# State products of four chunks issued as one group over four row groups in a chunked gated-recurrence layer

## Chip, cores and metric

One Trainium2 chip, all 8 cores, each with 4 of the 32 sequences; no core talks to another. The metric is the device time of the slowest core in microseconds (us). PE is TensorE (the matmul engine), DVE is VectorE, ACT is ScalarE, POOL is GpSimd, SP is the engine that issues most transfers.

## The reference, cut to what matters

One layer on x (32, 2048, 1024) in float32. A token-mixing half: a modulated RMSNorm, one input projection to q, forget logits, v, output gate and pooling values, then a gated recurrence in four heads of 128 channels, and a pooling mixer; both go through the output projection. A channel-mixing half: RMSNorm, up projection to 4096, squared ReLU, down projection. The part around the change, with chunks of 32 tokens:

```python
k_out = k * jnp.exp(b_last - b)              # decay from s to chunk end
def step(S, xs):
    q_c, k_c, v_c, d_c = xs
    o = jnp.einsum('bhcd,bhde->bhce', q_c, S)
    S = d_c[..., None] * S + jnp.einsum('bhcd,bhce->bhde', k_c, v_c)
    return S, o
```

The state product k_c^T v_c contracts over only the 32 tokens of a chunk and gives 128 x 128 per head. The products of different chunks do not depend on each other; the update of S does.

## The kernel before

Each core works through 8192 tokens in 16 tiles (t = 0 to 15) of 512 tokens. A tile is four blocks (j) of 128 tokens, a block four chunks (c = 4j + jj) of 32 tokens. The work of a tile:

- N1: RMSNorm and transposes into `ucT` (`norm_to_T`).
- A: input projection; per head the decays; `koutT` transposed to `koutk` (tokens on partitions), `scT` (scores), `qin`; v and the pooling values token by token (`vtok`, `ptok`).
- B (`stage_B`): `pool_j` and `pool_g` (the pooling mixer, PSUM banks 6 and 7), then for each block `chain(j)` and `oT(j)`. `chain` forms for each chunk the four heads' state products (PE, rows `pb<-vtok,koutk`), updates the float32 state with four multiply-adds (DVE, `S<-S,decs,pb`), and casts the state to bfloat16 (ACT, `Sbf<-S`). `oT` forms the block's outputs from scores and states (PE, rows `pb<-scT,vtok` and `pb<-qin,Sbf`), squares them (ACT, `osq`), averages over a head with a matmul by ones (PE, `pb<-osq,cbt`), takes Ln and Exp (ACT, `rsb`), and multiplies (DVE, `rsb<-pb,rsb`, the last read of the output's bank, then `ucT<-rsb,gnwc,sg`).
- C: output projection from `ucT` (PE, rows `pb<-wsl,ucT` with 512 columns) and gated residual add.
- N2: norm and transposes into `u2T`.
- UP: 32 groups of eight matmuls (`pb<-u2T,wsl`), each followed by a ReLU in place on DVE (`pb<-pb`) and a square on ACT (`hidT<-pb`). DOWN: 256 matmuls (`pb<-wsl,hidT`). OUT: final norm and store.

UP and DOWN use PSUM banks 0 to 3 in turn, everything of the mixing half banks 4 to 7. In `chain` the banks of the products alternate between 4 and 5 by chunk; `oT` puts its output into bank 6 or 7 and the averages into bank 4 or 5.

The order on each engine is not written by hand. The program lists its operations with their reads, writes, an assumed duration (`dur`) and a priority (`P.base`, then place in the list); a list scheduler (`Prog.schedule`) then simulates the engines and picks on each, whenever it is free, the ready operation of lowest priority value. Tile t+1's mixing half (base 10(t+1)) and tile t's UP and DOWN (base 10t + 15) are in play together, so MLP matmuls fill PE wherever the mixing half waits; the mixing half goes first where both are ready. Every PSUM bank is one buffer to the scheduler: a group that writes it waits for the last reader of what was there. The order found is fixed in the program; on the chip each engine runs it in order and waits on semaphores. Weights come through two rings of four slots (`wsl`), from float32 in the first tile (with a conversion by POOL's transfers) and from a bfloat16 copy afterwards. Only tile 0's mixing half has no MLP work beside it, and only tile 15's MLP has no mixing half.

Many operations are recorded by helpers: L480 is `mm` (all matmuls but transposes), L483 `tr`, L486 `actf`, L490 and L491 `ts`, L494 `tt`, L497 `stt`, L500 `cp`.

Of the kernel before, what the change touches and what calls it, by code (L numbers as in the profile page):

```python
# [17 lines left out]
TT = 512  # L18
# [281 lines left out]
def V(t, off, dims, p0=0, n=128):  # L300
    row = 1
    for s in t.shape[1:]:
        row *= s
    return bass.AP(t, p0 * row + off, [[row, n]] + [list(d) for d in dims])
# [23 lines left out]
def build_nc(NT=NT_FULL):  # L328
# [32 lines left out]
    with ExitStack() as st:  # L361
        def sb(name, shape, dt):
            return st.enter_context(nc.sbuf_tensor(name, list(shape), dt))
# [15 lines left out]
        vtok = sb("vtok", [128, 4, TT], BF16)  # L379
# [3 lines left out]
        koutk = sb("koutk", [128, 4, TT], BF16)  # L383
# [29 lines left out]
        pb = [st.enter_context(nc.psum_tensor("pb%d" % i, [128, 512], F32)) for i in range(8)]  # L413
# [13 lines left out]
        P = Prog()  # L427

        def bufs(name, n, **k):
            return [Buf("%s%d" % (name, i), **k) for i in range(n)]  # L430
# [15 lines left out]
        B_v = bufs("v", 4)  # L446
# [3 lines left out]
        B_koutk = bufs("koutk", 4)  # L450
# [9 lines left out]
        B_pb = bufs("pb", 8, excl=True)  # L460
# [18 lines left out]
        def mm(out, lhsT, rhs, start, stop, **k):  # L479
            return lambda e: e.matmul(out, lhsT=lhsT, rhs=rhs, start=start, stop=stop, **k)  # L480
# [4 lines left out]
        def actf(out, in_, func, **k):  # L485
            return lambda e: e.activation(out=out, in_=in_, func=func, **k)  # L486
# [6 lines left out]
        def tt(out, in0, in1, op):  # L493
            return lambda e: e.tensor_tensor(out=out, in0=in0, in1=in1, op=op)  # L494

        def stt(out, in0, s, in1, o0, o1):
            return lambda e: e.scalar_tensor_tensor(out=out, in0=in0, scalar=s, in1=in1, op0=o0, op1=o1)  # L497

        def cp(out, in_):
            return lambda e: e.tensor_copy(out=out, in_=in_)  # L500
# [5 lines left out]
        MS = 0.0585  # L506
# [257 lines left out]
        def stage_B(t):  # L764
            P.label = "B%d" % t
            first = t % 4 == 0

            def pool_j(j):
                first128 = first and j == 0
                bp = 6 + j % 2  # L770
                ps_, pp_ = (4 * t + j) % 5, (4 * t + j - 1) % 5
                fns = []
                rb = [B_p[ps_]]
                for g in range(4):
                    fns.append(mm(V(pb[bp], g * 128, [[1, 128]]), V(ptok, ps_ * TT + g * 128, [[1, 128]]),
                                  BAND((4 + g) if first128 else g), True, first128, skip_group_check=True))
                    if not first128:
                        fns.append(mm(V(pb[bp], g * 128, [[1, 16]]), V(ptok, pp_ * TT + g * 128, [[1, 128]]),
                                      BAND(8 + g, 16), False, True, skip_group_check=True))
                if not first128:  # L780
                    rb.append(B_p[pp_])
                P.pe(fns, reads=rb + C("cbt"), writes=[B_pb[bp]], dur=8 * MS)
                P.dve(cp(plv(j * 512, [[1, 512]]), pb[bp][:]), reads=[B_pb[bp]], writes=[B_E[j // 2]], dur=0.69)

            def pool_g(g):
                bx = 6 + g % 2
                P.pe([mm(V(pb[bx], 0, [[128, 4], [1, 128]]), V(wpool, g * 128, [[1, 128]]), plv(g * 128, [[512, 4], [1, 128]]),
                         True, True)], reads=B_E + C("wpool"), writes=[B_pb[bx]], dur=MM)
                P.act(actf(V(ucT, (4 + g) * TT, [[1, TT]]), pb[bx][:], AF.Copy, scale=V(psc, g, [[1, 1]])),
                      reads=[B_pb[bx]] + C("psc"), writes=B_uc[4 + g], dur=0.69)  # L790

            svs = {}

            def chain(j):
                if first and j == 0:
                    s0 = state["s32"] % 2
                    v0 = state["sbf"] % NSB
                    P.pool(lambda e: e.memset(V(S32, s0 * TT, [[1, TT]]), 0.0), writes=[B_S32[s0]])
                    P.pool(lambda e: e.memset(V(Sbf, v0 * TT, [[1, TT]]), 0.0), writes=[B_Sbf[v0]])
                for jj in range(4):  # L800
                    c = 4 * j + jj
                    bd = 4 + c % 2
                    svs[c] = state["sbf"] % NSB
                    P.pe([mm(V(pb[bd], h * 128, [[1, 128]]), V(koutk, h * TT + j * 128, [[1, 128]], p0=32 * jj, n=32),
                             V(vtok, j * TT + h * 128, [[1, 128]], p0=32 * jj, n=32), True, True, tile_position=(32 * jj, 0))
                          for h in range(4)], reads=B_koutk + [B_v[j]], writes=[B_pb[bd]], dur=4 * MS)
                    a, z = state["s32"] % 2, (state["s32"] + 1) % 2
                    state["s32"] += 1
                    P.dve([stt(V(S32, z * TT + h * 128, [[1, 128]]), V(S32, a * TT + h * 128, [[1, 128]]),
                               V(decs, h * 16 + c, [[1, 1]]), V(pb[bd], h * 128, [[1, 128]]), ALU.mult, ALU.add)  # L810
                           for h in range(4)], reads=[B_pb[bd], B_S32[a]] + B_dec, writes=[B_S32[z]], dur=1.4)
                    state["sbf"] += 1
                    v = state["sbf"] % NSB
                    P.act(actf(V(Sbf, v * TT, [[1, TT]]), V(S32, z * TT, [[1, TT]]), AF.Copy), reads=[B_S32[z]],
                          writes=[B_Sbf[v]], dur=0.63)

            def oT(j):
                bo = 6 + j % 2
                fns = []
                for h in range(4):  # L820
                    fns.append(mm(V(pb[bo], h * 128, [[1, 128]]), V(vtok, j * TT + h * 128, [[1, 128]]),
                                  V(scT, h * TT + j * 128, [[1, 128]]), True, False, skip_group_check=True))
                    for jj in range(4):
                        fns.append(mm(V(pb[bo], h * 128 + jj * 32, [[1, 32]]), V(Sbf, svs[4 * j + jj] * TT + h * 128, [[1, 128]]),
                                      V(qin, h * TT + j * 128 + jj * 32, [[1, 32]]), False, jj == 3, skip_group_check=True))
                P.pe(fns, reads=[B_v[j]] + B_scT + [B_Sbf[svs[4 * j + jj]] for jj in range(4)] + B_qin, writes=[B_pb[bo]],
                     dur=4 * 0.16)
                P.act(actf(osq[:], pb[bo][:], AF.Square, scale=CQ), reads=[B_pb[bo]], writes=[B_osq], dur=0.6)
                bm = 4 + j % 2
                P.pe([mm(pb[bm][:], ONES(), osq[:], True, True)], reads=[B_osq] + C("cbt"), writes=[B_pb[bm]], dur=MM)  # L830
                P.act(actf(rsb[:], pb[bm][:], AF.Ln, bias=epsc[:]), reads=[B_pb[bm]] + C("eps"), writes=[B_rsb], dur=0.69, aset="B")
                P.act(actf(rsb[:], rsb[:], AF.Exp, scale=-0.5), reads=[B_rsb], writes=[B_rsb], dur=0.63, aset="B")
                P.dve(tt(rsb[:], pb[bo][:], rsb[:], ALU.mult), reads=[B_pb[bo], B_rsb], writes=[B_rsb], dur=0.69)
                P.dve(stt(V(ucT, j * 128, [[TT, 4], [1, 128]]), V(rsb, 0, [[128, 4], [1, 128]]), gnwc[:],
                          V(sg, j * 128, [[TT, 4], [1, 128]]), ALU.mult, ALU.mult),
                      reads=[B_rsb] + C("gnwc") + B_sg, writes=[B_uc[k][j] for k in range(4)], dur=0.75)

            for j in range(4):
                pool_j(j)
            for g in range(4):  # L840
                pool_g(g)
            chain(0)
            oT(0)
            chain(1)
            oT(1)
            chain(2)
            oT(2)
            chain(3)
            oT(3)
# [135 lines left out]
```

How the kernel before makes its waits and increments, by code:

```python
            def run(e, eng):  # L265
                for i in prog.ops[e]:
                    o = ops[i]
                    for key, val in plan[i]:
                        eng.wait_ge(esem[key[1]] if key[0] == "e" else dsem[key[1]], val)
                    for f in o.fns:
                        ins = f(eng)
                    if o.dma_key is not None:
                        ins.then_inc(dsem[o.dma_key], 16)
                    elif o.signal:
                        ins.then_inc(esem[e], 1)
                if e == "sp":
                    for k in final_dma_keys:
                        eng.wait_ge(dsem[k], 16 * prog.dma_counts[k])
```

## Time and profile before

| what | value |
|---|---|
| median of the runs | 3151.07 us (lowest 3140.67) |
| the profiled execution | 3158.05 us |
| its span on the slowest core (core 4) | 3156.5 us |
| spans of the eight cores | 3120.8 to 3156.5 us |
| mean granted TensorE clock, core 4 | 0.959 |
| PE busy | 2904.8 us (92%) |
| DVE busy | 1718.4 us (54%) |
| ACT busy | 1411.3 us (45%) |

The busy time of PE counts each matmul's modelled latency, merged where they overlap; what a matmul costs in a stream is read from start to start. The granted clock is a share of 2.4 GHz; 0.5 means 1.2 GHz. A row of the timeline merges neighbours of one kind; its second number runs from the first start to the last modelled end, so it overlaps the next row. A few matmul records are missing, so a row's count can be one or two short.

### The profile page before, as it was taken

The page shows a single profiled execution, that of the slowest core. Times are in us where ns is not written, and L with a number is a line of the kernel's source. Part 1 is how long each engine was busy: PE and PEld are TensorE (multiplying, and loading weights), DVE is VectorE, ACT ScalarE, POOL GpSimd, SP SyncE. Part 2 cuts the span into 40 slices and gives each one's busy share as a digit, 9 for nine tenths or more (in the row PEclk, how much of TensorE's full clock was granted, in tenths as well). Part 3 has the DMA queues.
Part 4 walks back from the last instruction along what each step waited for, and adds up shares of the span by engine and source line. Part 5 has one row for each costly group of instructions (what it writes and reads, how often), then busy time and mean ns, then how long its engine had stood idle before and what let it go on. Part 6 is the DMA issues. An engine that isn't in the chain of part 4 may idle for free.

```text
span 3156.5 us, 49557 instructions; the slowest of 8 cores (3120.8 to 3156.5 us)
## 1 busy us (share of the span) xinstructions
PE 2904.8 (92%) x17236; PEld 1479.4 (47%) x17552; DVE 1718.4 (54%) x3278; ACT 1411.3 (45%) x2468; POOL 54.0 (2%) x74
## 2 busy tenths in 40 slices
PE   2168979999999999999999999999999999999998
PEld 1035435445454544545454554545454454545443
DVE  1146616647565664746565564746466474746541
ACT  3036406446362645536263643636264453626320
POOL 2000110000000000000000000000000000000000
PEclk9579999999999999999999999999999999999987
DMA  9964896363634535363543635353453636345243
GB/s 190 167 127 118 166 218 202 118 201 115 213 122 142 203 122 198 112 207 112 178 170 128 206 122 199 116 204 131 141 194 124 203 114 207 121 147 192 97 160 114
DMA packets 177506, 498.52 MB, mean 158 GB/s; under 512 B 15968, under 2 KB 65376, under 8 KB 177264
## 3 DMA queue, kind: packets, MB, share of 16 engines
q1 hardware_dynamic: 126752, 457.88, 42.5%
q0 software_dynamic: 50512, 37.46, 9.4%
q8 instruction: 146, 2.39, 0.3%
q14 instruction: 96, 0.79, 0.1%
HBM read 475.03 MB, written 57.70 MB: 169 GB/s over the span
## 4 chain that ended last, share of the span: by engine, by line
PE 86%; DMA 7%; issue 2%; ACT 2%; another core or an unknown queue 2%; DVE 1%; POOL 0%; DVEq 0%; ACTq 0%; SPq 0%; POOLq 0%
PE pb L480 84%; PE pb L483 2%; DMA wsl<-w_in 2%; DMA wsl<-w_down 2%; DMA hidT<-w_ada 1%; ACT ucT L486 1%; DMA wdn_s<-wsl 1%; DMA xh<-x 1%; DMA out<-xh 1%; ACT Sbf L486 1%; DVE S L497 0%; DVE xh L497 0%; ACT hidT L486 0%; DMA wsl<-wup_s 0%
## 5 line engine op out<-in xcount | busy, mean ns | idle before, releaser
L480 PE MATMUL pb<-u2T,wsl 128*128 128x512 bf16 x3950 | 946.2, 389 | 19.0 <-ACT hidT L486 5.5
L480 PE MATMUL pb<-wsl,hidT 128*128 128x512 bf16 x3990 | 922.1, 384 | 23.1 <-DMA wsl<-w_down 16.0
L480 PEld LDWEIGHTS pb<-wsl,hidT 128*128 128x128 bf16 x4096 | 393.6, 99 | 494.9 <-issue 74.3
L480 PEld LDWEIGHTS pb<-u2T,wsl 128*128 128x128 bf16 x4096 | 394.1, 100 | 476.8 <-issue 78.9
L490 DVE TENSOR_SCALAR pb<-pb 128x512 f32<-128x512 f32 x512 | 348.1, 695 | 282.7 <-PE pb L480 275.8
L480 PE MATMUL pb<-wsl,ucT 128*128 128x256 bf16 (+1 forms) x3054 | 471.9, 310 | 7.2 <-DMA wsl<-w_in 5.9
L494 DVE TENSOR_TENSOR pb<-pb,gbc 128x512 f32<-128x512 f32 x256 | 174.5, 695 | 533.4 <-PE pb L480 498.4
L486 ACT ACTIVATE hidT<-pb 128x512 bf16<-128x512 f32 x512 | 298.4, 595 | 235.2 <-DVE pb L490 234.0
L480 PEld LDWEIGHTS pb<-wsl,ucT 128*128 128x128 bf16 x3072 | 298.0, 98 | 155.0 <-issue 13.6
L486 ACT ACTIVATE hidT<-xh 128x1024 bf16<-128x1024 f32 x64 | 67.4, 1053 | 616.0 <-PE pb L480 612.7
L480 PE MATMUL pb<-ucT,wsl 128*128 128x512 bf16 x1504 | 334.6, 381 | 3.9 <-DMA wsl<-w_in 2.4
L497 DVE SCALAR_TENSOR_TENSOR S<-S,decs,pb 128x128 f32<-128x128 f32 x1024 | 286.3, 342 | 63.0 <-PE pb L480 57.9
L486 ACT ACTIVATE Sbf<-S 128x512 bf16<-128x512 f32 x256 | 158.9, 627 | 213.2 <-DVE S L497 213.2
L480 PEld LDWEIGHTS pb<-ucT,wsl 128*128 128x128 bf16 x1536 | 150.4, 98 | 185.9 <-issue 10.3
L486 ACT ACTIVATE xn<-xh 128x1024 bf16<-128x1024 f32 x128 | 134.9, 1054 | 138.3 <-DVE xh L494 112.9
L494 DVE TENSOR_TENSOR xh<-xh,pb 128x512 f32<-128x512 f32 x256 | 171.1, 683 | 12.1 <-DVE pb L494 0.5
L486 ACT ACT_TABLE_LOAD x98 | 125.7, 1283 | 106.6 <-PE pb L480 90.9
L480 PE MATMUL pb<-vtok,koutk 32*128 32x128 bf16 x1024 | 94.4, 220 | 21.8 <-DVE S L497 12.2
L490 DVE TENSOR_SCALAR xn<-xh,rst 128x1024 bf16<-128x1024 f32 x128 | 91.5, 748 | 38.8 <-ACT rst L486 38.8
L480 PEld LDWEIGHTS pb<-vtok,koutk 32*128 32x128 bf16 x1024 | 55.1, 94 | 102.1 <-issue 101.0
L491 DVE TENSOR_SCALAR fg<-ta,omlh,lbp 128x512 f32<-128x512 f32 x64 | 34.0, 545 | 121.2 <-ACT ta L486 121.1
L710 DVE TENSOR_TENSOR_SCAN xn<-scanm_t,ta 128x512 f32<-128x512 bf16 x64 | 76.4, 1215 | 33.7 <-ACT ta L486 33.7
(82 smaller groups left out, 1943.9 us busy)
## 6 DMA issues: line engine op xcount, KB each, us to landing
wsl<-wup_s SPq DMA_DIRECT2D x240, 512.0 KB, 4.7
wsl<-wdn_s SPq DMA_DIRECT2D x240, 512.0 KB, 3.6
wsl<-win_s SPq DMA_DIRECT2D x150, 512.0 KB, 3.4
xh<-x SPq DMA_DIRECT2D x64, 512.0 KB, 7.6
out<-xh SPq DMA_DIRECT2D x64, 512.0 KB, 6.8
wsl<-wout_s SPq DMA_DIRECT2D x60, 512.0 KB, 4.1
hidT<-w_ada POOLq DMA_DIRECT2D x12, 1024.0 KB, 35.4
wsl<-w_up POOLq DMA_DIRECT2D x16, 512.0 KB, 9.3
```

Source lines behind the costliest of these rows:

```text
L480: return lambda e: e.matmul(out, lhsT=lhsT, rhs=rhs, start=start, stop=stop, **k)
L483: return lambda e: e.transpose(out, in_, idn)
L486: return lambda e: e.activation(out=out, in_=in_, func=func, **k)
L490: return lambda e: e.tensor_scalar(out=out, in0=in0, scalar1=s1, scalar2=None, op0=o0)
L491: return lambda e: e.tensor_scalar(out=out, in0=in0, scalar1=s1, scalar2=s2, op0=o0, op1=o1)
L494: return lambda e: e.tensor_tensor(out=out, in0=in0, in1=in1, op=op)
L497: return lambda e: e.scalar_tensor_tensor(out=out, in0=in0, scalar=s, in1=in1, op0=o0, op1=o1)
L710: P.dve(lambda e: e.tensor_tensor_scan(out=bbv(x, 0, [[1, TT]]), data0=scanm[:], data1=ta[x][:], initial=0.0, op0=ALU.mult, op1=ALU.add), ...
```

## The change

In `chain`, the state products of all four chunks of a block are issued first, as one group of sixteen matmuls, head by head and within a head over the four row groups of the array (`tile_position=(32 * jj, 0)`, as before), each chunk into a bank of its own, 4 to 7. The group's assumed duration is 0.45 us in place of four times 4 x 0.0585. The four updates and casts follow as before, each reading its chunk's bank. In `oT` the output goes always to bank 4 and the averages to bank 5.

```diff
+                P.pe([mm(V(pb[4 + jj], h * 128, [[1, 128]]), V(koutk, h * TT + j * 128, [[1, 128]], p0=32 * jj, n=32),
+                         V(vtok, j * TT + h * 128, [[1, 128]], p0=32 * jj, n=32), True, True, tile_position=(32 * jj, 0))
+                      for h in range(4) for jj in range(4)], reads=B_koutk + [B_v[j]], writes=B_pb[4:8], dur=0.45)
                 for jj in range(4):
                     c = 4 * j + jj
-                    bd = 4 + c % 2
+                    bd = 4 + jj
                     svs[c] = state["sbf"] % NSB
-                    P.pe([mm(V(pb[bd], h * 128, [[1, 128]]), V(koutk, h * TT + j * 128, [[1, 128]], p0=32 * jj, n=32),
-                             V(vtok, j * TT + h * 128, [[1, 128]], p0=32 * jj, n=32), True, True, tile_position=(32 * jj, 0))
-                          for h in range(4)], reads=B_koutk + [B_v[j]], writes=[B_pb[bd]], dur=4 * MS)
...
             def oT(j):
-                bo = 6 + j % 2
+                bo = 4
...
-                bm = 4 + j % 2
+                bm = 5
```

The scheduler turns this into another order on every engine. PE, tile 3, from the pooling products (`pb<-Et,wpool_t`) to the first output group; `pb<-u2T,wsl` are UP's matmuls of tile 2. Before:

```order
L480 MATMUL pb<-u2T,wsl 128x512 x4
L480 MATMUL pb<-vtok,koutk 128x128 x4
L480 MATMUL pb<-Et,wpool_t 128x512 x4
L480 MATMUL pb<-vtok,koutk 128x128 x4
L480 MATMUL pb<-scT,vtok 128x128
L480 MATMUL pb<-qin,Sbf 128x32 x4
```

In the changed kernel:

```order
L480 MATMUL pb<-Et,wpool_t 128x512 x2
L480 MATMUL pb<-u2T,wsl 128x512 x8
L480 MATMUL pb<-Et,wpool_t 128x512
L480 MATMUL pb<-u2T,wsl 128x512 x4
L480 MATMUL pb<-Et,wpool_t 128x512
L480 MATMUL pb<-u2T,wsl 128x512 x8
L480 MATMUL pb<-vtok,koutk 128x128 x16
L480 MATMUL pb<-u2T,wsl 128x512 x24
L480 MATMUL pb<-wsl,hidT 128x512 x8
L480 MATMUL pb<-scT,vtok 128x128
```

MLP matmuls stand between the pooling products now, and the state products of block 0 come after them.

PE, the same tile, around the average of an output group (`pb<-osq,cbt`) and the state products of the next block. Before, of block 1:

```order
L480 MATMUL pb<-u2T,wsl 128x512 x8
L480 MATMUL pb<-osq,cbt 128x512
L480 MATMUL pb<-wsl,hidT 128x512 x4
L480 MATMUL pb<-vtok,koutk 128x128 x8
L480 MATMUL pb<-wsl,hidT 128x512 x12
```

In the changed kernel, of block 0:

```order
L480 MATMUL pb<-wsl,hidT 128x512 x8
L480 MATMUL pb<-osq,cbt 128x512
L480 MATMUL pb<-wsl,hidT 128x512 x12
L480 MATMUL pb<-vtok,koutk 128x128 x16
L480 MATMUL pb<-wsl,hidT 128x512 x28
L480 MATMUL pb<-scT,vtok 128x128
```

A group of state products follows the average of the block before by 12 MLP matmuls, and its own output group follows by 28.

DVE, tile 3, from the casts of the pooling (`Et<-pb`) through the state updates; `pb<-pb` are the MLP's ReLUs. Before:

```order
L500 CAST Et<-pb 128x512
L497 SCALAR_TENSOR_TENSOR S<-S,decs,pb 128x128 x4
L500 CAST Et<-pb 128x512 x2
L497 SCALAR_TENSOR_TENSOR S<-S,decs,pb 128x128 x4
L500 CAST Et<-pb 128x512
L497 SCALAR_TENSOR_TENSOR S<-S,decs,pb 128x128 x4
L490 TENSOR_SCALAR pb<-pb 128x512
L497 SCALAR_TENSOR_TENSOR S<-S,decs,pb 128x128 x4
L490 TENSOR_SCALAR pb<-pb 128x512 x4
```

In the changed kernel:

```order
L500 CAST Et<-pb 128x512
L490 TENSOR_SCALAR pb<-pb 128x512
L500 CAST Et<-pb 128x512 x2
L490 TENSOR_SCALAR pb<-pb 128x512 x2
L500 CAST Et<-pb 128x512
L490 TENSOR_SCALAR pb<-pb 128x512 x4
L497 SCALAR_TENSOR_TENSOR S<-S,decs,pb 128x128 x8
L490 TENSOR_SCALAR pb<-pb 128x512
L497 SCALAR_TENSOR_TENSOR S<-S,decs,pb 128x128 x4
```

All casts and seven ReLUs come before the first update, then two chunks' updates stand together.

## Rows read from the trace of the kernel before

**Rows 1.** Page, part 1: busy time, share of the span, instructions.

```profile
PE 2904.8 (92%) x17236; PEld 1479.4 (47%) x17552; DVE 1718.4 (54%) x3278; ACT 1411.3 (45%) x2468; POOL 54.0 (2%) x74
```

**Rows 2.** Stretches: length, busy of PE, PEld, DVE, ACT, POOL, clock, DMA share, GB/s.

```profile
1030.00:1230.00 200.00, 195.81 (x1158) 99.70 (x1179) 116.66 (x219) 99.10 (x175) 0.00 (x0) 0.99 0.50 180
```

**Rows 3.** Timeline of PE, tile 15: start, length, operation, count, [idle before, releaser].

```profile
2919.79 0.38 PE L480 MATMUL pb<-Et,wpool_t 128*128 128x512 bf16 x1 [0.20 <-ACT ucT L486]
```

**Rows 4.** Timeline of PE, tile 3, from the pooling products on.

```profile
744.96 0.60 PE L480 MATMUL pb<-Et,wpool_t 128*128 128x512 bf16 x2
746.28 0.38 PE L480 MATMUL pb<-Et,wpool_t 128*128 128x512 bf16 x1 [0.71 <-ACT ucT L486]
746.86 0.38 PE L480 MATMUL pb<-Et,wpool_t 128*128 128x512 bf16 x1 [0.20 <-ACT ucT L486]
747.49 0.38 PE L480 MATMUL pb<-vtok,koutk 32*128 32x128 bf16 x4 [0.26 <-DVE S L497]
748.68 0.22 PE L480 MATMUL pb<-scT,vtok 128*128 128x128 bf16 x1 [0.81 <-ACT Sbf L486]
...
749.79 1.86 PE L480 MATMUL pb<-u2T,wsl 128*128 128x512 bf16 x4 [0.33 <-ACT hidT L486]
...
754.12 0.39 PE L480 MATMUL pb<-vtok,koutk 32*128 32x128 bf16 x4
```

**Rows 5.** Timeline of PE, tile 3: MLP matmuls alone, then before a state group.

```profile
717.90 1.89 PE L480 MATMUL pb<-u2T,wsl 128*128 128x512 bf16 x8
719.63 1.91 PE L480 MATMUL pb<-wsl,ucT 128*128 128x256 bf16 x16
...
757.47 1.90 PE L480 MATMUL pb<-u2T,wsl 128*128 128x512 bf16 x8
759.30 0.39 PE L480 MATMUL pb<-vtok,koutk 32*128 32x128 bf16 x4
759.62 1.90 PE L480 MATMUL pb<-u2T,wsl 128*128 128x512 bf16 x8
```

**Rows 6.** Timeline of PE, tile 3: two chunks' products side by side.

```profile
764.52 1.02 PE L480 MATMUL pb<-wsl,hidT 128*128 128x512 bf16 x4
765.47 0.48 PE L480 MATMUL pb<-vtok,koutk 32*128 32x128 bf16 x8
765.89 2.76 PE L480 MATMUL pb<-wsl,hidT 128*128 128x512 bf16 x12
```

**Rows 7.** Stretches: the nine microseconds of rows 4 (columns as in rows 2).

```profile
745.00:754.00 9.00, 6.46 (x41) 2.71 (x41) 4.72 (x12) 7.32 (x13) 0.00 (x0) 0.81 0.17 60
```

**Rows 8.** Timeline, all engines: state updates in a row (tile 0), and from osq on.

```profile
217.13 1.12 DVE L497 SCALAR_TENSOR_TENSOR S<-S,decs,pb 128x128 f32<-128x128 f32 x4
...
218.49 1.12 DVE L497 SCALAR_TENSOR_TENSOR S<-S,decs,pb 128x128 f32<-128x128 f32 x4 [0.24 <-DVE S L497]
...
774.29 0.38 PE L480 MATMUL pb<-osq,cbt 128*128 128x512 bf16 x1
...
776.28 0.69 DVE L494 TENSOR_TENSOR rsb<-pb,rsb 128x512 f32<-128x512 f32 x1 [5.18 <-ACT rsb L486]
```

**Rows 9.** Timeline of PE, tile 0.

```profile
208.47 0.27 PE L480 MATMUL pb<-scT,vtok 128*128 128x128 bf16 x1 [1.02 <-ACT Sbf L486]
...
213.11 0.58 PE L480 MATMUL pb<-vtok,koutk 32*128 32x128 bf16 x4 [3.63 <-ACT rsb L486]
...
237.93 0.22 PE L480 MATMUL pb<-scT,vtok 128*128 128x128 bf16 x1
```

**Rows 10.** Waits: engine, line, awaited, us in total, times, longest.

```profile
PE pb L480 <- DMA wsl<-w_down: 16.0, 10, 4.9
```

**Rows 11.** Timeline of PE, tile 1: a late group and what followed.

```profile
349.86 0.53 PE L480 MATMUL pb<-vtok,koutk 32*128 32x128 bf16 x4 [1.82 <-ACT rsb L486]
350.34 4.22 PE L480 MATMUL pb<-u2T,wsl 128*128 128x512 bf16 x12
```

## The prediction

> **What bounds the kernel now.** I read the page first. TensorE (PE) is busy 92% of the span [rows 1], but its busy time is a model of pipelined matmuls, so I asked the table by stretch next: in a 200 us window of the steady part PE is busy 195.81 us at a granted clock of 0.99, VectorE 116.66 us and ScalarE 99.10 us [rows 2]. Nothing else comes near, so in the steady part every microsecond of PE time counts, and a wait on another engine counts only where PE has no other work queued. The period of one tile of 512 tokens comes from the timeline: the last pooling matmul of two tiles stands at 746.86 and, twelve tiles later, at 2919.79 [rows 3, 4], which is 181.1 us a tile. Then I looked, start to start, at what PE pays for the state products, and where it stands still around them. The third reading is the program's order, for what stands between a wait and its releaser.
>
> **The price of a state group now.** Eight 128x512 matmuls take 719.63 - 717.90 = 1.73 us, 0.216 each [rows 5]. The same eight in front of a state group take 759.30 - 757.47 = 1.83, so the change to 32-row tiles costs 0.10, and the group of four holds PE 759.62 - 759.30 = 0.32 more [rows 5]: 0.42 us for one chunk, of which only 4 x 0.054 (a quarter of 0.216) is streaming. Where two chunks already stand side by side, in different row groups and banks, the pair costs 765.89 - 764.52 - 4 x 0.216 = 0.51 [rows 6]: the second chunk adds 0.09. A tile has 12 lone chunks and 2 pairs: 12 x 0.42 + 2 x 0.51 = 6.06 us.
>
> **The change, part by part.** The number of matmuls, weight loads, vector and scalar operations stays the same. What changes:
>
> 1. Sixteen matmuls in one group. No row shows four row groups in flight. The floor is a lone chunk's 0.42 (all four side by side, plus next to nothing); the top is no overlap, 0.42 + 12 x 0.054 = 1.07. I take what the pair shows, 0.42 + 3 x 0.09 = 0.69, because it is the nearest case: two row groups, two banks, the same operands. Four blocks: 2.76 us a tile against 6.06, so 3.3 us less. At the floor it would be 4.4, at the top 1.8.
>
> 2. The products of block 0 can no longer run beside the pooling, since all four mix banks are needed at once. Before, they did, and that filled VectorE's queue with state updates and pooling casts, so the ReLUs of the MLP came late and PE had no MLP work: from the first pooling matmul at 744.96 to the next state group at 754.12 there are 9.16 us [rows 4]. The work in it is 4 pooling matmuls (0.86), a state group (0.42), the output group of block 0 (about 0.64), 12 MLP matmuls (2.59) and one osq matmul (0.22), 4.73 in all. So 4.4 us are lost: 0.71 + 0.20 + 0.26 + 0.81 + 0.33 = 2.3 us of idle time named by the rows, and the rest is clock: the granted clock over this stretch is 0.81 [rows 7], so part of it ran at 1.2 GHz instead of 2.4, right after PE had gone thin, and four MLP matmuls at 749.79 took 1.86 us [rows 4] where four others take 1.02 [rows 6]. The changed order puts 20 MLP matmuls between the pooling products and 32 between the first state group and its output group, and on VectorE lets the ReLUs through before the chain. I expect this loss to go.
>
> 3. New waits. The next group needs the banks that oT reads last, so it now waits for the multiply into rsb. The ones matmul starts at 774.29 and that multiply ends at 776.28 + 0.69 = 776.97, so 2.68 us [rows 8]; the order puts the osq matmul and 12 MLP matmuls there, 13 x 0.216 = 2.81. That is covered, barely. Behind the waiting group in PE's queue stands all MLP work; whoever waits for PE then waits too. The chain itself: chunks in a row start 218.49 - 217.13 = 1.36 us apart on VectorE [rows 8], so four need 3 x 1.36 + 1.12 = 5.2, then one cast of 0.63 and some 0.2 for hand-overs, after 0.69 for the group: 6.7. PE has 28 MLP matmuls (6.05) plus the group (0.69), 6.7. Covered to within 0.2. In block 0 two ReLUs (0.7 each) stand between the chunks: 8.1 against 32 x 0.216 + 0.69 = 7.6, so 0.5. Together 0.5 + 3 x 0.2 = 1.1, say 1.2 us a tile. Below this nothing (all covered); above, see the second rival.
>
> 4. Stage B gets longer. Before, from the first pooling matmul to the last output group of a tile, 128 MLP matmuls stood in the order; now 212 do, 84 more, all taken from what followed. When the second norm's transposes begin, 100 of DOWN's matmuls are still to come (176 before), so the longer stage is hidden in tiles 1 to 15: the next UP starts when DOWN ends, as before. In tile 0 nothing covers it. There, block 0's output group stands at 208.47, the next state group at 213.11 after 3.63 us for rsb (a table load is in it), the last output group at 237.93 [rows 9]. In the new order the first group waits for the pooling, which I put 2 us ahead of 208.47 (an estimate); its output comes 6.7 + 0.2 later, so 5 us later than now, and each later block costs 0.7 for the output group, 3.9 for the average and rsb, and 6.9, so 11.5 us, and the last output group comes near 248, +10. Some of wout's matmuls are then already behind. I charge 8 us, bounds 0 and 12.
>
> **Sum.** Per tile 3.3 + 4.4 - 1.2 = 6.5 us; 15 tiles 97.5; less 8 for tile 0: 89.5. The profiled execution took 3158.05, so it gives 3068.5. The median of the runs is 3151.07, 7 lower, so I predict 3062. A part of the gain in tile 1 may be eaten, as PE waits for the first load of w_down 16.0 us in all [rows 10]; no range beyond 7 us for that. From floor to top of part 1 the time goes from 3046 to 3085.
>
> **Rivals.**
>
> A. The stretch loss stays, because the pooling still alternates PE and ScalarE and PE goes thin all the same. For it: the pooling still runs on two banks and its waits of 0.71 and 0.20 on ucT [rows 4] are ScalarE's time, not the chain's. Against: MLP matmuls stand between them now. It takes back 4.4 - 1.2 on 15 tiles, 48 us: 3110, inside 2%.
>
> B. No overlap of four row groups. For it: nothing in the rows; against: the pair at 0.51. 60 groups x (1.07 - 0.69) = 23 us: 3085.
>
> C. Full overlap. For it: within a chunk each weight load has to follow its predecessor's row group, and across row groups it does not; against: the second chunk's 0.09, where full overlap would make it almost zero. 60 x 0.26 = 16 less: 3046. The Trainium skill, "TensorE: Matmul & The Clock Gate", Part 3, states that matmuls in distinct row groups run side by side with some 4 ns between starts; by that rule the group is near the floor, and the pair in this trace does not agree.
>
> D. Slower: the wait for rsb. Each of 45 groups behind an output group (and 15 behind the pooling) now has a chain of four hand-overs in front of it. The rows show what a late one costs: 1.82 us of waiting at 349.86, and then twelve MLP matmuls in 4.22 us [rows 11] instead of 2.76 [rows 6]: 3.3 us together. On 60 groups that is 197 us against the gain of 97.5 and 8 lost: 3151 + 197 - 89.5 = 3259, slower by 3%. It decides from 89.5 / 60 = 1.5 us a group. Against it: the cover was counted above and fits. The skill's "TensorEngine Tiling (Array Packing)", Gotcha 1, warns that row tiling raises PSUM pressure; that is this rival, and no row here prices four banks.
>
> **Chances.** Forecast 0.50, A 0.21, B 0.10, C 0.10, D 0.09. A measurement of this kernel tells about 2% from no change, which is below 3088. The forecast, B (3085, so half of it) and C fall there, with a little of the forecast's own spread lost: 0.65. Within 2%: A, half of B, a weak D: 0.28. Slower: 0.07. The range takes the forecast with both ends of the group's price and reaches to A: 3025 (more of the thin stretches gone, full overlap) to 3125.
>
> **What would show it.** Right: a state group of sixteen followed by the next matmul after about 0.6 us; no idle time and no clock drop at the pooling; the period near 174.6 us; waits of PE on rsb under 0.3 us each in tiles 1 to 15; the last output group of tile 0 some 10 us later. Wrong: PE waiting on rsb or Sbf by a microsecond or more per group, or a clock under 0.95 around the pooling, or the period unchanged with shorter state groups.

## The result and the profile after

The changed kernel is faster by 3 to 4%. The ratio to the kernel before was 0.9687 with a 95% interval of 0.9618 to 0.9757, and in a later job, beside other kernels on one chip, 0.9634 (0.9612 to 0.9656). The medians over all runs of the first measurement, 3195.28 us against 3266.6 us, hold runs in which a whole die had a lower clock (the ratio and its interval leave them out), so that 3195.28 lies outside the range of 3025 to 3125 that I gave and yet says nothing of the change; the two other runs of the changed kernel took 3046.86 and 3048.09 us. The profiled execution took 3046.86 us, against 3158.05 us before.

First the page, part 1, which answers to [rows 1]. PE's modelled busy time fell by 106 us, VectorE's and ScalarE's rose slightly:

```profile
PE 2798.4 (92%) x17235; PEld 1440.7 (47%) x17552; DVE 1728.6 (57%) x3278; ACT 1431.2 (47%) x2468; POOL 54.5 (2%) x74
```

The timeline of PE in tile 3, from the pooling products on, answers to [rows 4]:

```profile
742.17 0.59 PE L480 MATMUL pb<-Et,wpool_t 128*128 128x512 bf16 x2
742.60 1.89 PE L480 MATMUL pb<-u2T,wsl 128*128 128x512 bf16 x8
744.33 0.38 PE L480 MATMUL pb<-Et,wpool_t 128*128 128x512 bf16 x1
...
745.41 0.38 PE L480 MATMUL pb<-Et,wpool_t 128*128 128x512 bf16 x1
...
757.27 2.75 PE L480 MATMUL pb<-wsl,hidT 128*128 128x512 bf16 x12
759.95 0.40 PE L480 MATMUL pb<-vtok,koutk 32*128 32x128 bf16 x16
760.29 6.22 PE L480 MATMUL pb<-wsl,hidT 128*128 128x512 bf16 x27
766.34 0.22 PE L480 MATMUL pb<-scT,vtok 128*128 128x128 bf16 x1
```

No row carries an idle time in brackets: MLP matmuls stand where PE stood still. The price of a group of sixteen is read as in [rows 5]: 759.95 - 757.27 = 2.68, less 12 x 0.216, is 0.09 for going in; 760.29 - 759.95 = 0.34 on top, so 0.43 us. That is what four products cost before. The stretch that answers to [rows 7], from the first pooling product on; I call it the thin stretch, for PE had little to do in it before:

```profile
742.00:751.00 9.00, 8.95 (x56) 4.03 (x56) 4.95 (x13) 5.68 (x10) 0.00 (x0) 1.00 0.37 127
```

PE is busy for 8.95 of 9 us in place of 6.46, at a granted clock of 1.00 in place of 0.81. The last pooling product of tile 15 gives the period, as with [rows 3]:

```profile
2837.30 0.38 PE L480 MATMUL pb<-Et,wpool_t 128*128 128x512 bf16 x1
```

(2837.30 - 745.41) / 12 = 174.3 us a tile, against 181.1. The waits of PE from 600 to 2800 us, that is in the steady part alone, are of another kind now. Before:

```profile
PE pb L480 <- ACT ucT L486: 11.0, 24, 0.7
PE pb L480 <- ACT Sbf L486: 10.0, 12, 0.9
```

After, the same stretch:

```profile
PE pb L480 <- DMA wsl<-wdn_s: 13.2, 12, 2.1
PE pb L480 <- DMA wsl<-wup_s: 6.0, 7, 1.9
PE pb L480 <- ACT rst L486: 4.3, 5, 1.4
...
PE pb L480 <- DVE rsb L494: 0.2, 1, 0.2
```

The wait for rsb, on which the slower rival stood, is 0.2 us in twelve tiles, and there is none on Sbf. PE instead waits once a tile for a weight slot of DOWN. That wait belongs to this order and not to the shorter tile alone: two kernels below with the same period have none (pairs behind the pooling) or 0.9 us of it in all (the longer assumed duration).

### The profile page after: what moved, and what is told of

It is laid out like the page before. It is cut to its first block, busy times and chain, and to the rows that moved or that the text cites. A ratio compares the mean times of both kernels' runs of the same rounds, so it can differ in the third digit from the quotient of the medians.

```text
span 3044.4 us, 49254 instructions; the slowest of 8 cores (3014.4 to 3044.4 us)
## 1 busy us (share of the span) xinstructions
PE 2798.4 (92%) x17235; PEld 1440.7 (47%) x17552; DVE 1728.6 (57%) x3278; ACT 1431.2 (47%) x2468; POOL 54.5 (2%) x74
## 4 chain that ended last, share of the span: by engine, by line
PE 80%; DMA 13%; DVE 2%; issue 2%; another core or an unknown queue 2%; ACT 1%; SPq 0%; DVEq 0%; POOL 0%; ACTq 0%; POOLq 0%
PE pb L480 78%; DMA out<-xh 3%; DMA hidT<-w_ada 3%; PE pb L483 2%; DMA xh<-x 2%; DMA wsl<-wup_s 1%; DMA wsl<-wdn_s 1%; DMA wsl<-w_down 1%; DMA wsl<-w_up 1%; DVE xh L497 1%; DMA wdn_s<-wsl 1%; DVE S L497 0%; DMA wsl<-w_in 0%; DVE pb L490 0%
## 5 line engine op out<-in xcount | busy, mean ns | idle before, releaser
L480 PE MATMUL pb<-u2T,wsl 128*128 128x512 bf16 x3954 | 918.9, 382 | 32.1 <-DMA wsl<-w_up 6.9
L480 PE MATMUL pb<-wsl,hidT 128*128 128x512 bf16 x3965 | 910.5, 379 | 30.0 <-DMA wsl<-wdn_s 13.9
L480 PE MATMUL pb<-wsl,ucT 128*128 128x256 bf16 (+1 forms) x3063 | 478.1, 313 | 7.1 <-DVE S L497 4.0
L494 DVE TENSOR_TENSOR rsb<-pb,rsb 128x512 f32<-128x512 f32 x64 | 44.2, 691 | 160.9 <-ACT rsb L486 160.8
L710 DVE TENSOR_TENSOR_SCAN xn<-scanm_t,ta 128x512 f32<-128x512 bf16 x64 | 76.4, 1214 | 33.7 <-ACT ta L486 33.7
L483 PE MATMUL pb<-cbt,xn 128*128 128x128 bf16 x1024 | 75.3, 226 | 8.8 <-DVE xn L490 5.6
```

The lines of the kernel that those rows point to most:

```text
L483: return lambda e: e.transpose(out, in_, idn)
L710: P.dve(lambda e: e.tensor_tensor_scan(out=bbv(x, 0, [[1, TT]]), data0=scanm[:], data1=ta[x][:], initial=0.0, op0=ALU.mult, op1=ALU.add), ...
```

## The experiments

All ratios are against the kernel before on the same chip. A period is worked out as above: the last pooling products of tiles 3 and 15 in the timeline, their difference over 12, on the slowest core. The medians over all eight cores, read in the same way, are 181.0 us before, 180.2 with the banks alone, 177.2 with the order alone, 177.8 with pairs, 174.1 with pairs behind the pooling, and 173.7 and 173.5 in the two profiles of the changed kernel.

**Banks alone.** The kernel before with its four groups of four, and the bank plan of the changed kernel:

```diff
-                    bd = 4 + c % 2
+                    bd = 4 + jj
...
-                bo = 6 + j % 2
+                bo = 4
...
-                bm = 4 + j % 2
+                bm = 5
```

> The bank plan of the changed kernel (chunk jj in bank 4 + jj, output in bank 4, average in bank 5), but four groups of four products as before. In its order the four pooling products again stand together with no MLP matmul between them, as before. Theory (the gain is the cheap group of sixteen plus the refilled thin stretch): neither is there, so the tile period stays at 180 to 182 us, the thin stretch with its clock drop stays, and the ratio to the kernel before is 0.995 to 1.01. Rival (the four banks by themselves free the updates from waiting for products): period under 178 us, ratio under 0.985. Rival (the wait for rsb in front of each first chunk costs by itself): PE waits on rsb over 1 us per block, ratio over 1.02.

Measured: 0.9992 (0.9971 to 1.0012), period 180.2 us. The timeline of PE in tile 3 shows the thin stretch again:

```profile
765.45 0.38 PE L480 MATMUL pb<-Et,wpool_t 128*128 128x512 bf16 x1 [0.71 <-ACT ucT L486]
766.03 0.38 PE L480 MATMUL pb<-Et,wpool_t 128*128 128x512 bf16 x1 [0.20 <-ACT ucT L486]
766.76 0.38 PE L480 MATMUL pb<-vtok,koutk 32*128 32x128 bf16 x4 [0.35 <-ACT ucT L486]
```

The clock drop that I expected there is only partly there. In this tile the nine microseconds from the first pooling product on ran at the full granted clock:

```profile
764.15:773.15 9.00, 7.22 (x57) 3.49 (x58) 5.20 (x13) 7.30 (x13) 0.00 (x0) 1.00 0.20 60
```

The same nine microseconds of tiles 3 to 14 had a lower clock in 8 of 12 tiles, 0.86 in the mean, against 12 of 12 and 0.80 in the kernel before. The period is 0.9 us shorter, which the whole time does not show. PE waits for rsb 0.2 us in all (600 to 2800 us), so both rivals fall: the four banks by themselves give next to nothing in the whole time, and the longer chain they force costs nothing.

**The order alone.** The kernel before, groups of four and bank plan kept; only the first chunk of a tile also waits for the pooling's banks:

```diff
-                          for h in range(4)], reads=B_koutk + [B_v[j]], writes=[B_pb[bd]], dur=4 * MS)
+                          for h in range(4)], reads=B_koutk + [B_v[j]],
+                         writes=[B_pb[bd]] + (B_pb[6:8] if c == 0 and t > 0 else []), dur=4 * MS)
```

> The kernel before, its bank plan and its groups of four kept, with one thing changed: in tiles 1 to 15 the first chunk's products also wait for the pooling's banks 6 and 7, so the chain starts behind the pooling. Theory (the thin stretch is lost because updates and casts fill VectorE's queue ahead of the ReLUs): the stretch refills, no clock drop there, period 176.5 to 177.5 us, ratio 0.978 to 0.985. Rival (the gain comes from the cheaper group alone, the stretch's loss just moves): period 180 us or more, ratio over 0.993.

Measured: 0.9787 (0.9750 to 0.9824), period 177.8 us, 0.3 above what I gave. The timeline of PE, tiles 3 and 15:

```profile
728.32 0.38 PE L480 MATMUL pb<-Et,wpool_t 128*128 128x512 bf16 x1
728.53 1.03 PE L480 MATMUL pb<-u2T,wsl 128*128 128x512 bf16 x4
729.40 0.38 PE L480 MATMUL pb<-Et,wpool_t 128*128 128x512 bf16 x1
...
2863.42 0.38 PE L480 MATMUL pb<-Et,wpool_t 128*128 128x512 bf16 x1
```

One added dependency, and no cheaper matmul anywhere, gives 2.1%. The period fell by 3.3 us and not 4.4, since the order also broke up the pairs (all 16 chunks of a tile stand alone now, 16 x 0.42 = 6.7 us against 6.06), and other waits, 1.0 us a tile, came in.

**The order inside the group.** The changed kernel, chunk by chunk:

```diff
-                      for h in range(4) for jj in range(4)], reads=B_koutk + [B_v[j]], writes=B_pb[4:8], dur=0.45)
+                      for jj in range(4) for h in range(4)], reads=B_koutk + [B_v[j]], writes=B_pb[4:8], dur=0.45)
```

> The changed kernel with the sixteen products issued chunk by chunk instead of head by head; nothing else differs, and the order of all other instructions is the same. Theory (full overlap needs neighbours in different row groups): the group holds PE about 0.6 to 0.7 us instead of 0.43, as the chunk-by-chunk pair of before cost 0.51 instead of 0.42; 64 groups x 0.2 = 13 to 17 us more than the changed kernel, ratio to before 0.973. Rival (the chip runs the four row groups side by side in whatever order they are issued): 0.43 to 0.45 us a group, ratio 0.969.

Measured: 0.9642 (0.9620 to 0.9665). The timeline of PE, tile 3:

```profile
744.67 2.75 PE L480 MATMUL pb<-wsl,hidT 128*128 128x512 bf16 x12
747.35 0.43 PE L480 MATMUL pb<-vtok,koutk 32*128 32x128 bf16 x16
747.72 6.22 PE L480 MATMUL pb<-wsl,hidT 128*128 128x512 bf16 x28
```

2.68 - 2.59 + 0.37 = 0.46 us, 0.03 more than head by head and far from the 0.6 to 0.7 I expected. The overlap does not need neighbours in different row groups; my theory fell, and the rival stands within 0.01 us of its upper figure. In time this kernel and the changed one cannot be told apart (64 x 0.03 = 2 us).

Why then did the pair of before cost 0.51? The starts of the single matmuls in the traces tell. That pair was two groups, issued one after the other, each with a wait of its own. Of the 24 such pairs between 600 and 2800 us on core 4, 22 have the second chunk's first product 0.10 to 0.20 us behind the first chunk's (0.10 in [rows 6]), and in all 24 the next matmul comes 0.31 us after it. In the single group here the first products of neighbouring chunks start 0.013 us apart. So the 0.09 was the late start of a second group, and not the price of its products. Whether its wait or its issue holds it back is not shown.

**Pairs.** The kernel before with two chunks per group, banks 4 and 5, head by head:

```diff
+                    if jj % 2 == 0:
+                        P.pe([mm(V(pb[4 + q], ...), ..., tile_position=(32 * (jj + q), 0))
+                              for h in range(4) for q in range(2)], reads=B_koutk + [B_v[j]], writes=B_pb[4:6], dur=0.45)
```

> The kernel before with the products of two chunks issued as one group of eight, head by head over two row groups, in banks 4 and 5; output and average in the banks of before. Theory: a group of eight costs 0.43 like a group of sixteen or four, so eight groups a tile cost 3.4 us against 6.06 before and 1.7 in the changed kernel; the order puts MLP matmuls between the pooling products for the most part, so most of the 4.4 us of the thin stretch returns too: period 175 to 177 us, ratio 0.968 to 0.98. Rival (only groups over all four row groups overlap fully): 0.5 us or more a group. Tile 0 has output groups earlier than in the changed kernel, which may give back some microseconds.

Measured: 0.9845 (0.9824 to 0.9866), slightly worse than expected, period 178.8 us. A group of eight costs PE 0.42 us, so the group's price was right; what I had wrong is the stretch. The order puts MLP matmuls between the pooling products, but the second pair stands among them, and the stall moved behind it. The timeline of PE, tile 4:

```profile
911.48 0.40 PE L480 MATMUL pb<-vtok,koutk 32*128 32x128 bf16 x8
911.81 0.39 PE L480 MATMUL pb<-Et,wpool_t 128*128 128x512 bf16 x1
914.13 1.61 PE L480 MATMUL pb<-u2T,wsl 128*128 128x512 bf16 x4 [1.94 <-ACT hidT L486]
```

and the waits of PE from 600 to 2800 us say that it comes once a tile:

```profile
PE pb L480 <- ACT hidT L486: 23.2, 12, 1.9
```

**Pairs behind the pooling.** The same, with the first pair waiting for banks 6 and 7:

```diff
-                              ..., writes=B_pb[4:6], dur=0.45)
+                              ..., writes=B_pb[4:6] + (B_pb[6:8] if c == 0 and t > 0 else []), dur=0.45)
```

> Groups of eight in banks 4 and 5, and in tiles 1 to 15 the first group behind the pooling. Theory (the two parts add: 0.42 us per group start, 4.4 us per thin stretch): eight groups x 0.42 = 3.4 us a tile against 6.7 for the groups of four behind the pooling, whose period was 177.8, so 174.5 to 175 us; ratio to before 0.966 to 0.971, within 0.4% of the changed kernel. Rival (the wait for rsb and the longer chain of the changed kernel cost it what grouping gives): this one, where output has banks of its own, is faster than the changed kernel, period under 173.5 us. Rival (pairs as such are slow, as the 178.6 us of the pairs beside the pooling could say): 177 us or more.

Measured: 0.9653 (0.9622 to 0.9683), period 174.4 us: the first theory, both figures just under its lower ends. The two parts add. It issues eight groups a tile where the changed kernel issues four, 1.7 us more, and comes out level in the period, since it hardly waits for weights (0.8 us in all against 19.2). The waits of PE from 600 to 2800 us, the largest:

```profile
PE pb L480 <- DVE xh L494: 6.8, 12, 0.8
```

**The changed kernel again**, in the job with the pairs behind the pooling and the next two.

> The changed kernel once more, as the measure for the three that run beside it. Theory: ratio to before 0.965 to 0.970 (its profile gave a period of 173.6 to 174.1 us against 180.9, and chunk by chunk gave 0.9642 in the last job).

Measured: 0.9634 (0.9612 to 0.9656), just past the end I gave; profiled at 3028.53 us, period 173.8 us.

**Tile 0 as before.**

```diff
-                    bd = 4 + jj
+                    bd = 4 + jj if t > 0 else 4 + c % 2
...
-                bo = 4
+                bo = 4 if t > 0 else 6 + j % 2
...
-                bm = 5
+                bm = 5 if t > 0 else 4 + j % 2
```

(and in tile 0 the groups of four of before).

> The changed kernel with tile 0's chain and outputs as before (groups of four, banks 4 and 5, output in 6 or 7); tiles 1 to 15 as changed. Theory (the serial chain has no cover in tile 0): from tile 0's first pooling product to tile 1's, 114 to 117 us as before instead of 125 to 139, of which a part is lost again to the first loads of weights; 5 to 12 us less than the changed kernel, ratio to before 0.962 to 0.966. Rival (the first loads set the pace of the first tiles anyway): less than 3 us, the first stretch up to tile 3 as long as in the changed kernel.

Measured: 0.9636 (0.9602 to 0.9670), the same as the changed kernel, but with an interval of 10 us to either side the time cannot tell 5 to 12 us from less than 3. The traces can. The first pooling products of tiles 0 and 1 in the timeline of PE, first in the changed kernel beside it, then here:

```profile
197.10 0.59 PE L480 MATMUL pb<-Et,wpool_t 128*128 128x512 bf16 x2 [1.16 <-DVE Et L500]
322.41 0.59 PE L480 MATMUL pb<-Et,wpool_t 128*128 128x512 bf16 x2
```

```profile
202.74 1.01 PE L480 MATMUL pb<-Et,wpool_t 128*128 128x512 bf16 x2
318.46 0.59 PE L480 MATMUL pb<-Et,wpool_t 128*128 128x512 bf16 x2
```

From one to the other pass 125.3 and 115.7 us, and all eight cores agree (124.3 to 125.4 against 114.7 to 116.2). Up to tile 3 each core keeps some of it, 7.9 us in the mean. So the serial chain of tile 0 costs about 8 us in the traces, as the theory had it, and the rival does not hold there. What of it the slowest core's time keeps is not resolved by these runs.

**Another transfer rate for the scheduler**, on top of tile 0 as before:

```diff
-DMA_RATE = 300e3
+DMA_RATE = 200e3
```

> As the changed kernel with tile 0 as before, and the scheduler's assumed transfer rate 200 instead of 300 GB/s, which only moves the order (MLP matmuls come some 12 later against the mixing half). Theory (in the changed kernel PE waits 13.9 us for weights of DOWN and 6 us for UP since the order uses four slots in a row sooner than they land): those waits drop by half or more, 8 to 15 us less, ratio 0.957 to 0.962. Rival (the slots are refilled as late whatever the order, since they are freed by PE itself): waits on the weights stay over 15 us, ratio as with tile 0 alone.

Measured: 0.9680 (0.9643 to 0.9717). The waits for weights did go, all of them, but PE now waits 28.7 us in 49 places for the norm's input to the transposes (from 600 to 2800 us):

```profile
PE pb L483 <- DVE xn L490: 28.7, 49, 1.6
```

The wait changed its name, and the time did not get better: the theory is wrong, and so is the rival, which had the waits for weights stay.

**DOWN in the program's order**, on top of tile 0 as before:

```diff
+        B_dn = Buf("dn")
...
-                             reads=[B_w[wi]] + [B_hid[k] for k in ks], writes=[B_pb[j]], dur=4 * MM)
+                             reads=[B_w[wi]] + [B_hid[k] for k in ks], writes=[B_pb[j], B_dn], dur=4 * MM)
```

> The changed kernel with tile 0 as before, and DOWN's groups kept in the order of the program (weight slot by weight slot over the four banks; before, the scheduler let bank 0 run through four slots in a row where the second half begins). Theory (PE waits 1.1 us a tile for DOWN's weights because one bank eats four slots in 16 matmuls): those waits are gone or under 3 us in all, and PE waits on the gated adds (VectorE, pb and xh) by less; 6 to 14 us less than with tile 0 alone, ratio 0.958 to 0.962. Rival (the adds free the banks too slowly, 1.4 us each): the wait changes its name, ratio 0.963 to 0.968.

Measured: 0.9742 (0.9713 to 0.9770), slower than either expectation. The waits of PE from 600 to 2800 us:

```profile
PE pb L480 <- DVE S L497: 19.6, 12, 1.6
PE pb L480 <- DVE xh L494: 8.6, 13, 0.8
```

The waits for DOWN's weights are gone and 28 us on VectorE stand in their place. Where they stand, the timeline of PE in tile 3 shows:

```profile
763.58 1.02 PE L480 MATMUL pb<-wsl,hidT 128*128 128x512 bf16 x4 [0.68 <-DVE xh L494]
766.23 1.86 PE L480 MATMUL pb<-wsl,ucT 128*128 128x512 bf16 x4 [1.63 <-DVE S L497]
```

The smaller wait is DOWN's second half waiting for a gated add. The larger one is not DOWN's: the output projection (`pb<-wsl,ucT`), next in the order, needs a bank that a state product still holds, and the updates that free it take turns on VectorE with the gated adds. Letting bank 0 run ahead, as the scheduler had it, gives the shorter time.

**A longer assumed duration of the group.**

```diff
-                      ..., writes=B_pb[4:8], dur=0.45)
+                      ..., writes=B_pb[4:8], dur=16 * MS)
```

> The changed kernel with the group of sixteen assumed to take 0.94 us instead of 0.45 in the scheduler; the program is the same but for the order, which puts four MLP matmuls fewer between a group and its output group. Theory (the chain of updates is covered with some 0.2 us to spare at 28 MLP matmuls, and no more): PE waits on Sbf by 0.3 to 0.9 us a block in tiles 1 to 15, 20 to 45 us in all, ratio 0.970 to 0.978. Rival (the assumed duration does not matter, since the queue of PE is deep enough): ratio within 0.002 of the changed kernel, 0.9634.

Measured: 0.9633 (0.9611 to 0.9655), as the changed kernel. I had read the order carelessly: only block 0 of a tile has four MLP matmuls fewer (28 in place of 32) between group and output, the other blocks have the same number, so the experiment is narrower than its expectation says. For block 0 it is clear. The timeline of PE, tile 3, shows the shorter distance and no wait:

```profile
728.96 0.40 PE L480 MATMUL pb<-vtok,koutk 32*128 32x128 bf16 x16
729.29 5.36 PE L480 MATMUL pb<-u2T,wsl 128*128 128x512 bf16 x24
734.48 1.03 PE L480 MATMUL pb<-wsl,hidT 128*128 128x512 bf16 x4
735.34 0.22 PE L480 MATMUL pb<-scT,vtok 128*128 128x128 bf16 x1
```

So there was more cover in block 0 than I had counted. And the wait for DOWN's weights, 13.2 us in the changed kernel, is 0.9 here, with 9.1 us for UP's weights, 8.2 for xh and 6.0 for xn instead (600 to 2800 us): once more other names for the same time.

## Why the prediction was right or wrong

Direction and mechanism were right; the size was short. I forecast 3062 us, a ratio of 0.972 to the median of 3151.07. The two runs behind the first ratio took 3047 and 3048, those of the later job 3028 to 3034, ratio 0.963. Step by step:

*Part 1, the group's price: the mis-sized term.* I took 0.69 us, extending the pair's 0.42 to 0.51 by 0.09 per chunk. It measured 0.43, the floor but for 0.01, and chunk by chunk 0.46. 60 groups x 0.26 = 16 us, and rival C was the right one here. The step that failed is "the nearest case": the pair's extra 0.09 was not a price per chunk but the late start of a second group (see the order inside the group). Four groups of 0.43 are 1.7 us a tile, so 4.3 less than before and not 3.3. The rule of the Trainium skill that I had weighed and put at 0.10, "TensorE: Matmul & The Clock Gate", Part 3 (matmuls in distinct row groups run side by side), agrees with the trace: sixteen products hold PE 0.43 us where four held it 0.42, and in the changed kernel neighbours in different row groups start 0.003 to 0.004 us apart. The pair of before, which I had held against the rule, does not speak against it.

*Part 2, the thin stretch: right.* The order alone gives 2.1%, almost three fifths of the later job's 3.7%, though not one matmul in it is cheaper. That the place of the first group causes it held in three ways: banks alone kept the waits, and most of the clock drops, and gained next to nothing; pairs beside the pooling moved it to where PE waits for the MLP's squares (hidT) again, 1.94 us a tile; and wherever the first group stood behind the pooling it was gone. Rival A is excluded. What is less sure is the queue that I blamed. The timeline of all engines before, tile 3:

```profile
746.24 1.11 DVE L497 SCALAR_TENSOR_TENSOR S<-S,decs,pb 128x128 f32<-128x128 f32 x4
747.27 1.88 DVE L490 TENSOR_SCALAR pb<-pb 128x512 f32<-128x512 f32 x3
747.91 1.14 ACT L486 ACTIVATE Sbf<-S 128x512 bf16<-128x512 f32 x2
748.95 0.59 ACT L486 ACTIVATE hidT<-pb 128x512 bf16<-128x512 f32 x1
```

The ReLUs do wait behind state updates on VectorE, but the squares then wait behind two casts of the state on ScalarE, which is busy 7.32 of the nine microseconds in [rows 7] and 5.68 after, while VectorE has 4.72 and 4.95. Both queues hold the MLP back; no run tells their shares apart.

*Part 3, the new waits: wrong in kind, and too small.* I priced 1.2 us a tile, all of it for Sbf. It is nil. The updates of a block, in the timeline of all engines:

```profile
760.50 2.34 DVE L497 SCALAR_TENSOR_TENSOR S<-S,decs,pb 128x128 f32<-128x128 f32 x8
...
763.01 1.12 DVE L497 SCALAR_TENSOR_TENSOR S<-S,decs,pb 128x128 f32<-128x128 f32 x4 [0.17 <-DVE S L497]
...
764.31 1.12 DVE L497 SCALAR_TENSOR_TENSOR S<-S,decs,pb 128x128 f32<-128x128 f32 x4 [0.17 <-DVE S L497]
...
765.53 0.63 ACT L486 ACTIVATE Sbf<-S 128x512 bf16<-128x512 f32 x1 [0.67 <-DVE S L497]
```

From the group's start at 759.95 to the cast's end at 766.16 are 6.2 us, not 6.7: the group is shorter, and chunks follow at 1.23 to 1.30 us, not 1.36, which was read in tile 0. The output group at 766.34 finds its state ready. In their place came the waits for weights and statistics, (13.2 + 6.0 + 4.3) / 12 = 2.0 us a tile, 2.3 with the smaller ones. Rival D, the slower one, fell with the rsb wait. The two attempts at those waits did not win the time: each time a wait on VectorE stood in their place.

*The period adds up.* Take the 181.1 of before less 6.06 for groups and 4.4 for the stretch: 170.6. With 6.7 for groups and (3.6 + 3.1 + 2.8 + 2.2) / 12 = 1.0 for the waits of its own, the order alone should have 178.3 (177.8 measured). With 3.4 and 0.9, pairs behind the pooling should have 174.9 (174.4). With 1.7 and 2.0, and some smaller waits, the changed kernel should have 174.6 (174.3, and 173.8 in the later job); my forecast of the period was 174.6. The other cores' periods differ from the slowest core's by up to 1.4 us, so the sum is no finer than that. Where the stall is still there the sum needs the clock as a term of its own. The mean granted clock in the nine microseconds from the first pooling product on is 0.86 with the banks alone and 0.87 with pairs, which costs some 9 x 0.14 = 1.3 and 9 x 0.13 = 1.2 us: banks alone 170.6 + 6.4 + 2.0 + 1.3 = 180.3 (180.2), pairs 170.6 + 3.4 + 3.4 + 1.2 = 178.6 (178.8).

*Near by luck in part.* The period came out as forecast because two errors cancel: the groups give 1.0 us a tile more than I had, and the waits take 1.1 more. That rival C's 3046 is the measured time within 2 us has the same reason; that rival is borne out by the 0.43 and not by the time.

*Part 4, tile 0: near in size.* I put the last output group near 248 and charged 8 us. The timeline of PE, tile 0:

```profile
207.64 0.26 PE L480 MATMUL pb<-scT,vtok 128*128 128x128 bf16 x1 [4.82 <-ACT Sbf L486]
...
213.80 0.62 PE L480 MATMUL pb<-vtok,koutk 32*128 32x128 bf16 x16 [5.15 <-DVE rsb L494]
...
240.34 0.31 PE L480 MATMUL pb<-scT,vtok 128*128 128x128 bf16 x1
```

The waits I described are all there, 5.15 us for rsb among them, and a block takes (240.34 - 207.64) / 3 = 10.9 us where I had 11.5. Times from the start of the span mislead here, since the pooling itself starts at 204.19 in the one execution and at 198.70 in the other: counted from there the last output group comes at 33.7 us before and at 41.6 now, 7.9 later where I had 10. The experiment on tile 0 says 8 us as well, though the whole time does not resolve it. One count of mine was off: between the first pooling product and the last output group of a tile the traces have 112 MLP matmuls before and 192 now, not 128 and 212; the conclusion does not change.

*What is left.* Between the two profiled executions lie 111 us, of which 2172.93 - 2091.89 = 81 fall between tiles 3 and 15. About 20 more are no effect of the change that I can show: in the profiled execution of before the core's last part ran at a lower clock (core 4, from about 3020 us on), and from tile 15's last pooling product to its end it took 236.7 us, core 0 of the same execution 215.9. The rows below are two stretches of it in the windows of core 4, with columns as in [rows 2]:

```profile
3020.00:3030.00 10.00, 9.91 (x39) 4.14 (x39) 5.10 (x7) 3.50 (x6) 0.00 (x0) 0.81 0.88 299
...
3080.00:3120.00 40.00, 39.73 (x151) 16.53 (x152) 5.18 (x8) 0.00 (x0) 0.00 (x0) 0.81 0.35 120
```

The second window on core 0 in the same execution of the kernel before, at the full clock:

```profile
3080.00:3120.00 40.00, 40.00 (x187) 18.19 (x186) 6.11 (x10) 0.00 (x0) 0.00 (x0) 1.00 0.35 119
```

Whether the changed kernel has fewer such dips by design or by luck was not tried. I used that execution as the base of a sum whose terms came from elsewhere in it; the spans of its eight cores, 3120.8 to 3156.5, could have warned me. The fairer base is the later job, where the ratio is worth 0.0366 x 3146 = 115 us against my 89.5. The median periods of the eight cores fell by 7.5 us and not 6.5, which is 15 us over fifteen tiles; the other 10 or so I cannot assign.

## What to carry to other kernels

Look at the order before the arithmetic: more than half of this gain came from where the first state group stands, not from what it costs, and one added dependency in the old kernel finds almost three fifths of it. A list scheduler that lets the latency-bound work go first can starve the engines that feed the filler work; PE rows with idle times just behind a burst on VectorE and ScalarE, with a lower clock behind them, are the sign. Small 32-row products are paid here by the visit, not by the piece (0.42 us for four, 0.43 for sixteen), so put as many as banks allow in one group; and when a wait for transfers or for a drain is moved by hand, expect it to come back under another name and measure the whole.

## What the runs showed of the hardware that I had not expected

A visit to the 32-row tiles costs 0.42 us with four products of 128 columns, 0.42 with eight head by head, 0.43 with sixteen head by head and 0.46 with sixteen chunk by chunk; two groups of four one after the other took 0.51 in [rows 6]. Four products in one row group would stream in 4 x 0.054 = 0.22 us, so about half of the price of a visit is going in and out, which fits what the Trainium skill says in "TensorEngine Tiling (Array Packing)", Key Properties, that a change of tiling mode drains the array; 0.09 to 0.10 us of it is seen ahead of the group. That sixteen chunk by chunk cost less than the pair of before, 0.46 against 0.51, is a matter of starts: in all these groups the next full matmul starts 0.15 us behind the last product's start, and the pair's last product starts late, because its second group does. The order between the row groups costs the 0.03 that is left between 0.46 and 0.43.
